# Value products of two heads alternating on the two column halves of TensorE, with four buffers for the turned scores

## What is computed

```python
def causal_block_attention(q, k, v, cum=None):
    ...
        s = jnp.where(kpos[None, :] <= qpos[:, None], s, NEG_INF)
        p = jax.nn.softmax(s, axis=-1)
        return jnp.einsum('bhqk,bhkd->bhqd', p.astype(v.dtype), v)
...
for l in range(DEPTH):
    o_a = mla_branch(...)    # 8 heads, values 64 wide
    o_b = fox_branch(...)    # 8 heads, values 64 wide
    o_c = rwkv_branch(...)
```

## Time and profile before

| | |
|---|---|
| time, median of 3 executions | 1476.27 us (1476.21 to 1480.7) |
| span of the profiled execution | 1475.1 us |
| own time of the profiled execution | not listed apart from the three |
| TensorE busy | 1404.1 us, 95% |
| VectorE busy | 801.6 us, 54% |
| ScalarE busy | 568.3 us, 39% |

### The profile page before, as it was taken

One profiled execution on the slowest core, in us unless ns is written; L12 is line 12 of the kernel. 1 busy time (PEld: TensorE's weight loads), 2 busy tenths in 40 slices (PEclk: granted clock), 3 DMA queues, 4 the chain that ended last, 5 costly groups with the idle time before them and its releaser, 6 DMA issues.

```text
span 1475.1 us, 24626 instructions
## 1 busy us (share of the span) xinstructions
PE 1404.1 (95%) x10704; PEld 1015.7 (69%) x10704; DVE 801.6 (54%) x1186; ACT 568.3 (39%) x848; POOL 52.3 (4%) x43
## 2 busy tenths in 40 slices
PE   6999999999899999999899999988999999998898
PEld 6887454453796445444688787777788978877876
DVE  4766112211756121122777877677767886767764
ACT  4542111111442101111456476633546556764342
POOL 0010000000120000000000000010000000001000
PEclk9999999999999999999999999999999999999999
DMA  9448999999269999998344334410464433432032
GB/s 378 163 146 343 423 423 421 423 422 419 102 239 372 375 422 422 422 423 374 120 160 141 117 127 143 166 38 3 156 217 165 144 112 135 168 111 90 4 115 86
DMA packets 47490, 340.26 MB, mean 231 GB/s; under 512 B 5296, under 2 KB 5296, under 8 KB 7568
## 3 DMA queue, kind: packets, MB, share of 16 engines
q1 hardware_dynamic: 45504, 328.03, 57.3%
q0 software_dynamic: 1872, 10.57, 1.9%
HBM read 337.53 MB, written 1.05 MB: 230 GB/s over the span
## 4 chain that ended last, share of the span: by engine, by line
PE 79%; DVE 8%; ACT 7%; DMA 3%; issue 2%; DVEq 0%; SPq 0%
PE bank L541 47%; PE bank L904 14%; PE bank L945 7%; PE bank L848 4%; PE bank L547 3%; DMA ring<-wfirst 2%; ACT arena L1620 2%; ACT d_hi L1436 2%; DVE d_lo L1840 1%; ACT arena L1397 1%; PE bank L877 1%; PE bank L882 1%; DVE arena L2266 1%; DMA ring<-wsecond 1%; DVE arena L2415 1%
## 5 line engine op out<-in xcount | busy, mean ns | idle before, releaser
L1840 DVE TENSOR_TENSOR d_lo<-ring,d_hi 128x2048 fp32r<-128x2048 f32 (+2 forms) x111 | 249.3, 2255 | 110.7 <-ACT d_hi L1436 110.5
L1436 ACT ACTIVATE d_hi<-ring 128x2048 fp32r<-128x2048 f32 (+2 forms) x115 | 215.9, 1887 | 145.5 <-PE bank L541 114.8
L541 PE MATMUL bank<-arena 64*64 64x64 f32 (+7 forms) x3680 | 181.7, 235 | 20.0 <-ACT arena L1397 5.5
L541 PEld LDWEIGHTS bank<-arena 64*64 64x64 f32 (+4 forms) x3680 | 150.4, 139 | 47.1 <-issue 18.2
L1397 ACT ACTIVATE arena<-bank 128x512 f32<-128x512 f32 (+4 forms) x190 | 103.3, 552 | 188.4 <-PE bank L541 143.9
L541 PE MATMUL bank<-xT_hi,d_hi 128*128 128x256 f32 x592 | 167.3, 283 | 2.3 <-ACT arena L1716 1.7
L541 PE MATMUL bank<-xT_hi,d_lo 128*128 128x256 f32 x592 | 166.2, 281 | 0.0
L541 PE MATMUL bank<-d_hi,xT_hi 128*128 128x512 f32 (+1 forms) x400 | 158.9, 397 | 7.5 <-ACT arena L1658 4.0
L541 PE MATMUL bank<-xT_lo,d_hi 128*128 128x256 f32 x592 | 165.7, 280 | 0.0
L541 PE MATMUL bank<-d_hi,xT_lo 128*128 128x512 f32 (+1 forms) x400 | 158.1, 395 | 0.0
L541 PE MATMUL bank<-d_lo,xT_hi 128*128 128x512 f32 (+1 forms) x400 | 157.2, 393 | 0.0
(11 more groups left out here) (357 smaller groups left out, 2013.6 us busy)
## 6 DMA issues: line engine op xcount, KB each, us to landing
ring<-wmoe SPq DMA_DIRECT2D x84, 1024.0 KB, 17.7
ring<-wsecond SPq DMA_DIRECT2D x80, 1024.0 KB, 4.8
arena<-wmoe SPq DMA_DIRECT2D x72, 1024.0 KB, 18.1
ring<-wfirst SPq DMA_DIRECT2D x30, 1024.0 KB, 4.9
wide<-wmoe SPq DMA_DIRECT2D x24, 1024.0 KB, 20.2
xT_raw<-wmoe SPq DMA_DIRECT2D x12, 1024.0 KB, 20.5
rows<-lnrows POOLq DMA_DIRECT2D x4, 1024.0 KB, 7.4
ring<-wsecond SPq DMA_DIRECT2D x4, 848.0 KB, 10.7
```

Of the source, the lines that this page charges most:

```text
L541: mark(nc.tensor.matmul(o, lhsT, rhs, start=start, stop=stop, skip_group_check=loose), full)
L1436: nc.scalar.activation(high_of(u)[:, 0:width], raw[u % NRAW][:, 0:width], ACT.Copy).then_inc(sem("piece_high"), 1)
L1840: v.tensor_tensor(d_lo[u % NRAW][:, 0:width], raw[u % NRAW][:, 0:width], high_of(u)[:, 0:width], SUB).then_inc(sem("piece_low"), 1)
```

## The change

The products of two heads that share a bank are made together: 256 columns of the even head, 256 of the odd one, 128 of the even one, 128 of the odd one. For this four turned heads must fit, so `PT` gets a second pair of buffers (`PT_more`), and the turned scores go through banks 5, 6 and 7 in turn. TensorE's order is now: turn 0 to 3, products of heads 0 and 1, turn 4 and 5, products of 2 and 3, turn 6 and 7, products of 4 and 5, products of 6 and 7.

```diff
+        PT_more = ca(2, 3 * P)
...
+        def turned_head(h):
+            return (PT, PT_more)[h % 4 // 2][:, h % 2, :]
...
                 def turn_p(h):
                     if h % 4 == 0:
                         pe_eng.wait_ge(sem("p_ready"), pe.next("p_ready"))
-                    b = 5 + h % 2
+                    b = 5 + h % 3
                     pe_eng.wait_ge(bank_free[b], pe.reuse(b))
                     for t in range(3):
                         tr(banks[b][:, t * P:(t + 1) * P], Pm[:, h, t * P:(t + 1) * P], full=b if t == 2 else None)
-                turn_p(0)
-                for h in range(NH):
-                    if h + 1 < NH:
-                        turn_p(h + 1)
-                    pe_eng.wait_ge(bank_free[5 + h % 2], pe.used(5 + h % 2))
-                    ob = h // 2
-                    if h % 2 == 0:
-                        pe_eng.wait_ge(bank_free[ob], pe.reuse(ob))
-                    o = banks[ob][HC * (h % 2):HC * (h % 2) + HC, :]
-                    mm(o[:, 0:T], vn[:, 0, h, :], PT[:, h % 2, 0:T], stop=False, loose=True)
-                    mm(o[:, P:T], vn[:, 1, h, :], PT[:, h % 2, T:T + P], start=False, full=ob if h % 2 else None, loose=True)
+                    freed[h] = (b, pe.used(b))
+                def two_heads(ob):
+                    for h in (2 * ob, 2 * ob + 1):
+                        b, used = freed[h]
+                        pe_eng.wait_ge(bank_free[b], used)
+                    pe_eng.wait_ge(bank_free[ob], pe.reuse(ob))
+                    for at in range(2):
+                        for m in range(2):
+                            h, o = 2 * ob + m, banks[ob][HC * m:HC * m + HC, :]
+                            if at == 0:
+                                mm(o[:, 0:T], vn[:, 0, h, :], turned_head(h)[:, 0:T], stop=False, loose=True)
+                            else:
+                                mm(o[:, P:T], vn[:, 1, h, :], turned_head(h)[:, T:T + P], start=False, full=ob if m else None, loose=True)
+                for h in range(4):
+                    turn_p(h)
+                for ob in range(NH // 2):
+                    two_heads(ob)
+                    for h in (2 * ob + 4, 2 * ob + 5):
+                        if h < NH:
+                            turn_p(h)
...
             def turned_p(first=0, end=NH):
                 for h in range(first, end):
-                    b = 5 + h % 2
-                    copy_out(PT[:, h % 2, :], b, banks[b][:, 0:3 * P])
+                    b = 5 + h % 3
+                    copy_out(turned_head(h), b, banks[b][:, 0:3 * P])
```

More of the change, by code:

```diff
@@ L1035, in apply @@
             def apply(vn):
+                freed = {}
                 def turn_p(h):
```

## The result

The changed kernel takes 1464.77 us (median of four runs, 1464.29 to 1466.12), the kernel before in the same session 1476.33 (four runs, 1476.21 to 1480.7). The ratio is 0.9917, with a 95% interval of 0.9905 to 0.9929: 11.6 us less, where 12.6 were forecast. The profiled execution of the changed kernel took 1466.12 us.

A forecast was written before the change was run, and what follows sets the result against it. TensorE, busy 95% of the span, was taken as the bound. Pass gains 3.7 + 2.5 + 2.5 + 3.9 = 12.6 us off the 1475.1 span gave 1462.5, plus 1.2 to the median: 1463.7 us, 8-in-10 range 1461.0 to 1469.5.

The forecast's parts named there:

- Overlap, 2.6 a pass: Attention passes: two heads' products on different column halves run side by side, 0.65 us instead of 1.30, saving 2.6 a pass.
- strict order: Rival, chance 0.10: matmuls begin and end strictly in program order, so two heads cost 0.65 + 0.215 us; 1465.8 us total.
- no overlap: Rival, chance 0.06: a bank's two products don't overlap, only changes of shape are saved, 4.6 us in all; 1471.6 us.
- a drain at each change of half: Rival, chance 0.08: twelve changes of half per pass each drain the array; 1478.7 us at 0.15 each, 1483.5 at 0.25.
- Changes of tile shape, 1.2: Attention passes: seven groups of products become three, 14 shape changes become 6, saving 8 x 0.15 = 1.2 us a pass.
- Second attention, layer 0: 3.7, pass 6.7: Layer 0's second attention: the pass falls from 10.44 us to 6.7, a gain of 3.7.
- First attentions: 2.5 each, pass 7.5: Both layers' first attentions: pass 10.45 to 7.5 us with a 0.76 stall, then 0.4 wait for `v`; 2.5 left each.
- the rival that these passes give nothing: Rival, chance 0.08: tighter VectorE and ScalarE work behind the first attentions loses their 5 us; 1468.7 us.
- Second attention, layer 1: 3.9: Layer 1's second attention, 12.0 us before: 3.8, plus 0.3 of waits saved, less about 0.2 for a new wait; 3.9.
- I keep that stretch as it is: Layer 1's second attention: the half-clock stretch, 1294.0 to 1297.2 and adding 1.6 us, was assumed to stay after the change.
- The low part of `mg2`, which I had just in time: Layer 1's second attention: VectorE's low part ends at about 1301.4, TensorE wants it at 1301.5; 0.3 late if either is off.
- my signs of being wrong: Product groups keep 1.3 us, the clock stretch moves or multiplies, or some 2.5 us idle appears behind the first pass.

The follow-up runs named there:

- the changed kernel again: The changed kernel run once more with no edit: median 1466.41 us against 1478.46 for the kernel before beside it, ratio 0.9923.

## Why the prediction was right, and where its reasons were not

**Overlap, 2.6 a pass.** Measured by taking it away: 2.44. The size came from the experts' products and holds. The reason that I gave, that the products must alternate, doesn't: the order inside a pair is worth nothing. It was luck that this did no harm: the alternating order that I chose for it is one of two that give the same. What counts is that two heads on different halves are ready with no transposes between them. For the same reason strict order, the rival at 0.10, fails, and so do no overlap and a drain at each change of half: the latter needed 0.10 us for each, and twelve more of them a pass left it at 6.80, 0.1 from the forecast without any price.

**Changes of tile shape, 1.2.** Measured 1.20, so 0.15 each, as read from the difference of two rows, if all of the 1.20 is theirs.

**Second attention, layer 0: 3.7, pass 6.7.** 10.44 - 6.80 = 3.64.

**First attentions: 2.5 each, pass 7.5.** 2.92 less 0.38 behind it is 2.54, and 2.92 less 0.41 is 2.51. Both waits stood where they were put and with the size given, 0.74 for 0.76 at head 5 and 0.38 and 0.41 for 0.4 at `v`'s second piece. So the rival that these passes give nothing falls.

**Second attention, layer 1: 3.9.** This is the term that was mis-sized, and the step that failed in it is "I keep that stretch as it is". The half clock was not there after the change, and the old kernel has a profile without it too, with a pass of 11.08, and so has the old order with four buffers, 11.09. It had hidden two things. In the old pass it covered waits: I took 1.6 off the 12.0 for it and was left with 0.4 of waits, where at full clock the pass has 1.02, and the two profiles differ by 0.92 only. In the new pass it would have covered the wait behind the sigmoid. Head 3's copy came when I said, 4.6 us from the first transpose (1287.18 + 0.49 - 1283.06), but the pair was due at 1287.75 - 1.39 = 1286.36, 3.3 from it, and not at 4.4. So the wait was 1.39 and not 0.2. At full clock on both sides the term is 11.08 - 7.86 = 3.2. Between the two first profiles it is 12.00 - 7.86 = 4.1, and that this lies near 3.9 is luck of the clock. The low part of `mg2`, which I had just in time, was in time: from the end of the pass to the projection are 1.13 us (1290.92 to 1292.05).

**The sum.** 2.54 + 3.64 + 2.51 + 3.22 = 11.9, against 11.56 and, with the changed kernel again, 12.05 in the medians, each with an interval of about 1.8 to either side. From the second to the third pass the changed kernel needs 279.09 where the old one had 278.59, both without half clock. The other profiles of kernels in pairs that have none in that stretch lie at 278.80 to 279.29, and of the old order only one profile has none, so whether 0.2 to 0.7 are lost there or this is spread stays open.

**From span to median.** The median does not lie 1.2 over the span by nature. The changed kernel's profiled execution took 1466.12 with a span of 1463.9, so 2.2 lie around a span, and the old kernel's profiled execution must have taken some 1477.3, 1.0 above its median. Its fourth pass at half clock, 0.92 longer, would account for that. The forecast is the same as 1476.27 - 12.6. Of its miss of 1.1 us the sum explains 0.7, the step of layer 1's second attention, and the rest is well within the interval. One of my signs of being wrong was there, the clock's stretch did move; but it moves between two profiles of the kernel before as well, so it speaks neither for nor against the account.

**What stays open.** Behind the fourth pass, in layer 1's recurrent branch, half clock appears in six of the eleven profiles of kernels with products in pairs, and in none of three with the old order. That part takes 170.2 to 171.0 us without it, 171.9 to 174.0 with 3.4 us at half, and 174.4 to 174.7 with 10.2. In layer 0's branch it appears with both orders, and for 10.2 us only in two kernels with pairs, two buffers and both heads on one half. Whether shorter passes make it likelier behind the fourth pass, so few profiles can't tell. If they do, that is up to 4 us of an execution that the change gives back there. The medians, 11.6 to 12.05 us less, have whatever it costs in them.

## What to carry to other kernels

Where products use one half of the array's columns, two of them ran side by side here when both were ready and no transposes stood between: make the operands of two heads ready ahead, and don't mind the order inside the pair. The buffers and banks that allow this are worth nothing alone, and pairs without buffers next to nothing; it takes both. When TensorE gets faster, look through the other engines' lists for what is issued ahead of the copies it waits for: here a table load of 1.28 us with its work cost 0.7 to 0.8 us in three of the four passes, as the kernels with four copies ahead of it show, and moving one copy only moved the stall to the next one, so count the copies up to the one that the last group before the load needs.

## What the runs showed of the hardware

- TensorE ran products on two column halves side by side also when they were issued one head after the other: eight instructions in 0.88 us in either order, against 1.49 on one half.
- A change between the shapes 128*128 and 128*64 costs some 0.15 us: a pass with eight of them less was 1.20 us shorter (10.44 against 9.24, both heads on one half). That the 1.20 is all theirs is inferred.
- Two heads' products that followed each other on different halves took 1.45 us, a change of shape included, where the second head's copy ended only 0.60 behind the first head's start (kernel before, heads 6 and 7), and 0.80 where both were ready (changed kernel, heads 0 and 1).
- Stretches at half of 2.4 GHz, 3.4 to 10.2 us long, appear at other places in two profiles of one and the same kernel. They cost 0.9 us in a pass with waits, up to 4 in a recurrent branch, and nothing at 874.9 between two attentions (75.63 us with it, 75.64 without). A stage that is compared between two kernels is compared at the same granted clock.
